# Prompt attention's steps take up to four groups of probabilities, with their value products in the same step

## The reference, cut to what matters

```python
s = einsum(q, cmp_kv_k) - slopes * d_c        # 63 compressed blocks
p_cmp = masked_softmax(s, d_c >= 0)
s = einsum(q, ksel) - slopes * d_s            # selected blocks (all 16 of the prompt's)
p = masked_softmax(s, d_s >= 0)
s = einsum(q, win_k) - slopes * d_w           # the last 512 positions
o = g[0] * o_cmp + g[1] * o_slc + g[2] * o_win
```

## Time and profile before

| what | value |
|---|---|
| three runs | 1866.67, 1868.42, 1874.32 us (median 1868.42) |
| span of the profiled execution | 1866.5 us |
| time of the profiled execution | not given apart from its span; the span lies 0.2 us under the fastest run |
| PE, DVE, ACT, POOL busy, share of the span | 98%, 49%, 36%, 33% |
| `attend`, from its first transpose to the first product of the output projection | 549.9 to 889.2 us, 339.3 us |
| PE busy in that stretch | 319.8 us |

### The profile page before, as it was taken

How to read it: one execution, slowest core, us unless ns; L and a number is a source line. 1 busy time by engine, 2 the same in 40 slices (tenths; PEclk the granted TensorE clock), 3 DMA queues, 4 the chain that set the end, 5 groups by cost and what they waited for, 6 DMA issues and landing times.

```text
span 1866.5 us, 34543 instructions
## 1 busy us (share of the span) xinstructions
PE 1824.8 (98%) x13412; PEld 1708.9 (92%) x13412; DVE 915.0 (49%) x1630; ACT 665.8 (36%) x1249; POOL 615.2 (33%) x614
## 2 busy tenths in 40 slices
PE   8999989999998999999999999999999999999998
PEld 7999989999986766667999999999999999999998
DVE  6799965684557677767323221212121212125525
ACT  5312333345346666667323212121212121214435
POOL 2204972242304443445442222222222222125531
PEclk9999999999999999999999999999999999999999
DMA  4321476355423443441431111111111111113114
GB/s 153 127 68 46 117 206 148 92 150 124 137 64 96 138 137 104 125 137 54 142 133 46 34 57 35 57 38 54 40 51 40 52 40 51 40 46 97 57 35 139
DMA packets 186466, 163.62 MB, mean 88 GB/s; under 512 B 22068, under 2 KB 168176, under 8 KB 185783
## 3 DMA queue, kind: packets, MB, share of 16 engines
q1 hardware_dynamic: 175853, 138.06, 25.3%
q0 software_dynamic: 7840, 21.25, 4.2%
q10 hardware_dynamic: 2610, 2.10, 0.4%
HBM read 147.70 MB, written 18.25 MB: 89 GB/s over the span
## 4 chain that ended last, share of the span: by engine, by line
PE 61%; DVE 4%; issue 2%; POOL 2%; ACT 2%; ACTq 0%; POOLq 0%; DVEq 0%
PE ps L198 26%; PE ps L204 13%; PE ps L2345 5%; PE ps L1825 3%; PE ps L2724 3%; PE ps L1837 3%; PE ps L1813 2%; POOL S L1780 2%; PE ps L1864 2%; PE ps L2734 1%; DVE S L2074 1%; PE ps L2750 1%; PE ps L1900 1%; ACT S L1961 1%; PE ps L1872 1%
## 5 line engine op out<-in xcount | busy, mean ns | idle before, releaser
L184 POOL TENSOR_TENSOR wm_lo<-wm_raw,wm_hi 128x512 fp32r<-128x512 f32 (+1 forms) x96 | 169.7, 1768 | 543.6 <-ACT wm_hi L179 543.6
L2535 DVE TENSOR_TENSOR xT<-ps,xT 128x1056 f32<-128x1056 f32 x64 | 80.5, 1258 | 254.5 <-PE ps L204 254.5
L1780 POOL TENSOR_SCALAR S<-S,inv,gate_p 128x640 f32<-128x640 f32 (+7 forms) x186 | 124.9, 688 | 191.5 <-DVE inv L2084 191.5
L179 ACT ACTIVATE wm_hi<-wm_raw 128x512 fp32r<-128x512 f32 (+1 forms) x96 | 73.9, 770 | 281.4 <-PE ps L204 281.4
L198 PE MATMUL ps<-Ahi,wm_hi 128*128 128x352 f32 x768 | 164.9, 323 | 0.9 <-ACT wm_hi L179 0.9
L198 PE MATMUL ps<-Hhi,wm_hi 128*128 128x352 f32 x768 | 165.2, 323 | 0.0
L198 PE MATMUL ps<-Alo,wm_hi 128*128 128x352 f32 x768 | 164.6, 322 | 0.0
L198 PE MATMUL ps<-Hlo,wm_hi 128*128 128x352 f32 x768 | 164.6, 322 | 0.0
L1164 DVE SCALAR_TENSOR_TENSOR y<-u,conv_w,y 128x1024 f32<-128x1024 f32 x120 | 156.5, 1350 | 1.2
L2516 DVE SCALAR_TENSOR_TENSOR sq<-ps,rstd 128x1056 f32<-128x1056 f32 x32 | 40.2, 1258 | 225.1 <-PE ps L204 225.1
L1008 PE MATMUL ps_p<-Xhi,w1hi 128*128 128x256 f32 x544 | 138.7, 293 | 1.4 <-ACT Xhi L713 1.4
(11 more groups left out here) (431 smaller groups left out, 3830.3 us busy)
## 6 DMA issues: line engine op xcount, KB each, us to landing
s_raw<-in_cache_slc_kv_dram SPq DMA_DIRECT2D x256, 128.0 KB, 2.1
raw<-in_cache_cmp_kv_dram SPq DMA_DIRECT2D x132, 128.0 KB, 4.5
wm_raw<-in_w_up_dram SPq DMA_DIRECT2D x32, 512.0 KB, 4.1
wm_raw<-in_w_down_dram SPq DMA_DIRECT2D x64, 256.0 KB, 2.7
raw<-in_cache_cmp_kv_dram POOLq DMA_DIRECT2D x124, 128.0 KB, 4.5
win_raw<-in_w_in_dram SPq DMA_DIRECT2D x38, 256.0 KB, 3.3
wg_raw<-in_w_ple_gate_dram SPq DMA_DIRECT2D x14, 512.0 KB, 3.7
xT<-x_spill SPq DMA_DIRECT2D x2, 2112.0 KB, 8.4
```

Of the source, the lines that this page charges most:

```text
L179: self.c.nc.scalar.activation(self.hi[s][:, 0:nk, :], self.raw[rs][:, 0:nk, :], ACT.Copy).then_inc(self.hi_ready, 1)
L184: self.c.nc.gpsimd.tensor_tensor(self.lo[s][:, 0:nk, :], self.raw[s % self.raw_slots][:, 0:nk, :], self.hi[s][:, 0:nk, :].bitcast(F32), AL ...
L1780: nc.gpsimd.tensor_scalar(x, x, inv[:, n % 3, 3 * e + br:3 * e + br + 1], c.gate_p[:, i, H * br + h:H * br + h + 1], ALU.mult, ALU.mult).t ...
L2535: nc.vector.tensor_tensor(three(x), banks[s][:, :, 0:CH], three(x), ALU.add).then_inc(W.free, 1)
```

## The change

Two lines set the size of a step and the place of `pv`, one constant is new, and the loop behind the last step goes. Steps now hold up to four groups: 1, 1, 1, 2, 2, 2, 2, 2 steps for i = 0 to 7, so 52 in place of 88. NS, START, the score chunks for a step and the last steps' extra work follow from that by the same formulas: the quads now start between step 4 and step 41, two or three steps apart (before: four or five).

```diff
+STEP = 4
...
-    steps = [[m for m in range(a, min(a + 2, first_group[n + 1]))] for n in range(NU) for a in range(first_group[n], first_group[n + 1], 2)]
+    steps = [[m for m in range(a, min(a + STEP, first_group[n + 1]))] for n in range(NU) for a in range(first_group[n], first_group[n + 1], STEP)]
...
-                for k in (steps[st - 1] if st else ()):
+                for k in steps[st]:
                     pv(k)
...
-        for k in steps[-1]:
-            pv(k)
```

## The result

The change makes the kernel slower: 1996.41 us (median of four runs, 1993.88 to 2000.66) against 1869.76 us, a ratio of 1.0676 with a 95% interval of 1.0656 to 1.0697. The forecast was 1933 us with a range up to 1968 us: the sign was right, the size was about half of what came.

The account below looks back on a forecast made before the run. The prediction took PE, busy 319.8 of the attention stage's 339.3 us, as the bound. Cycles of 317 us plus quads' 83 and 6 us gave a 406 us stage, 67 us more, so 1933 us; range 1893 to 1968 us.

Parts of the forecast that it names:

- What bounds the kernel: Attention stage: PE busy 319.8 of 339.3 us, so reordering can win at most 19.5 us.
- The new waits of prompt attention: Attention stage: value products wait for copies, exponentials, mixA, DVE or POOL; a round takes 79.7 us instead of 58.3.
- cycle 1 to 2: From i = 1's first-step value products to i = 2's: DVE's inverse and reads delay the third chunk; 9.85 us against 5.9.
- i = 2 to 3: Between these units' first-step value products: six exponentials precede mixA on ACT; 9.0 us, PE alone needing 5.9.
- Page loads: covered.: Attention stage, SyncE: a quad's 16 pages take 13.4 us, quads come 17 us apart, so loads cost nothing.
- The clock as a rival: Attention stage: PE's clock falls after each of twelve long waits, 23 us more, 1956 us; chance 0.10.
- twelve waits of 3 us and more: Attention stage, PE: waits made by the change at 0 to 1, 1 to 2 and 2 to 3, in four rounds.
- sign of being wrong: Attention stage: forecast wrong if mixA's waits stay under 15 us, or the stage slows with PE's busy time grown.
- The sum: Whole kernel: stage 406 us instead of 339.3, 67 us more, giving 1933 us; chance 0.74.
- the two rivals: Attention stage: page loads bound it, 1880 us, chance 0.05; or PE's clock falls after waits, 1956 us, chance 0.10.
- Faster: Attention stage: larger steps shrink PE's waits for POOL and mixA, up to 15 us gained, 1852 us; chance 0.05.
- no change: Attention stage: gains and waits cancel, 1868 us; chance 0.06.

Follow-up runs that it names:

- mix_first: The changed kernel with mixA copied ahead of the late exponentials on ACT: 1964.3 us.
- weigh_late: The changed kernel with DVE's inverses behind the score reads in units of one step: 1963.9 us.
- loads_fixed: The changed kernel with each four cache pages read by one DMA from fixed places, leaving out the page table: 1968.6 us.
- early_value: The changed kernel with the value products of quads z = 0 and 9 in their fourth step instead of their fifth: 1982.1 us.
- filled: The changed kernel with the second score chunk of i = 3, 4 and 5 computed four, four and three times into the same place: 1972.9 us.
- place_only: The kernel before with only the value products moved into their own step, steps keeping two groups: 1921.0 us, ratio 1.0275.

## Why the prediction was right or wrong, point by point

- *What bounds the kernel; nothing but the stage changes.* Right. The rest of the program is the same to 1 us.
- *The new waits of prompt attention, 86 us where 19.5 were.* Right in kind and close in size: without pages they are 81.0 us (115.2 less 34.2). mixA, the mn wait behind the inverse, and POOL are all there. The forecast that mixA alone would make 40 us was not met (24.3), since mn took 33.1 in the same units; the prediction's own cycle 1 to 2 has DVE's reads end that wait. The three longest of these waits in the first round match: cycle less PE's own need is 4.6, 3.95 and 3.1 us in the prediction, and PE waited 4.63, 3.67 and 2.97 us. The causes are shown by mix_first and weigh_late, each of which takes its wait away.
- *Single cycles.* i = 1 to 2: forecast 9.85 us, seen 11.6 (564.29 to 575.92), in part at the low clock. i = 2 to 3: forecast 9.0 us, seen 10.2 (575.92 to 586.12). The exponentials took from 581.80 to 585.71, 3.9 us as forecast; the difference is in the value products of i = 2, 3.2 us for 1.8, at the low clock.
- *"Page loads: covered."* This step failed. It compared rates: 13.4 us of SyncE for a quad, one quad every 17 us. The rate was indeed enough over the stage; SyncE waited for PE for 157 us in the change. But a half buffer comes back only with the value product of the quad two or three before. With quads two or three steps apart there is little between this and the next use of the pages, and nothing behind the value products of z = 0 and 9; the way over issue (7 us) and landing (2 us) is longer than what PE has to do there. The round trip should have been held against the steps between release and use. It cost 34.2 us (loads_fixed, early_value).
- *The clock as a rival of 0.10 with 23 us.* The rival had the mechanism, its place and nearly its price, and came on top of the forecast instead of in its place: busy time grew by 32.0 us. This is the second step that failed: the sum lets PE's own work stay as it is and gives the clock nothing. The forecast itself held twelve waits of 3 us and more, in a stage where PE had never idled for over 1.9 us. Nothing in the rows said that such waits are free, the row near the start showed the low level, and the trace of the kernel before shows at 279 us what a wait of 3.48 us brings: eight transposes in 1.94 us, where 1.09 is the full-clock price. Of the twelve waits ten reach 3 us (eight on mn, two on mixA), two more on mixA are 2.97 and 2.58 us, and five page waits of over 3 us come with them. The prediction's own sign of being wrong, a slower stage with PE's busy time grown, came true. That the clock costs time by itself is shown by filled.
- *The sum.* 67 us forecast, 127.7 measured: 61.5 in waits of the forecast kind, 34.2 in waits for pages, 32.0 in busy time. The first is close to the forecast, and in part by luck: the prediction let a quad's PE work in the waits and its ACT work ahead of mixA cancel without working that out. The range ended at 1968 us because the two rivals were each put beside the forecast, never together with it.
- *Faster, no change.* Neither. The gain that they rested on exists, but is small: POOL's waits fall from 8.0 to 2.1 us in place_only, and 34.6 us come for mixA.

## What to carry to other kernels

When steps get longer, look on each in-order engine for what now stands in front of the small instruction that somebody waits for: a copy of 0.27 us behind exponentials cost more than 30 us. For each buffer count the steps between its release and its next use, not only the rate at which it is filled. And when a forecast holds idle stretches on PE that are longer than any in the trace, add what the clock does after them to the forecast, not to a rival.

## What the runs showed of the hardware

- Added matmul work can pay by the clock: 28 us of repeated matmuls (0.82 to 0.88 us each, 32 times) put in front of waits took the granted clock of the stage from 0.89 to 0.94 and made the kernel 23 us faster.
- Two stages with nearly the same idle time can have different clocks. weigh_late and mix_first last 434.9 and 435.7 us, with 102.1 and 93.9 us of PE idle. mix_first keeps the eight waits of up to 4.8 us on mn and has fourteen idle stretches of 3 us or more, a clock of 0.90 and 341.8 us of busy time; weigh_late has seven such stretches, 0.95 and 332.9 us.
- In the slow stretch behind the page wait eight transposes took 1.97 us against 1.09 us at full clock, and the windows row there reads a granted clock of 0.50.
- One DMA of a 128 KB page took 2.1 us from issue to landing (median, the change), one of four pages 5.9 us (loads_fixed).
